# The unit norm of the delta rule's queries, taken at the output norm

## The reference, cut to what matters

```python
def rms_norm(x, w):
    xf = x.astype(jnp.float32)
    y = xf * lax.rsqrt(jnp.mean(xf * xf, axis=-1, keepdims=True) + NORM_EPS)
    return (y * w.astype(jnp.float32)).astype(x.dtype)

def l2_normalize(x):
    xf = x.astype(jnp.float32)
    return xf * lax.rsqrt(jnp.sum(xf * xf, axis=-1, keepdims=True) + NORM_EPS)
...
    qkv = jax.nn.silu(causal_dwconv(qkv, qkv_conv))
    q, k, v = [...]
    o = gated_delta_rule_chunked(l2_normalize(q), l2_normalize(k), v, g, beta)
    o = rms_norm(o, o_norm) * jax.nn.silu(z...)
...
    qc = chunks(q) * (dk ** -0.5)        # in the delta rule: the only use of q
    attn = jnp.einsum('nbhik,nbhjk->nbhij', qc, kc) * decay
    ...
        o_c = (jnp.einsum('bhck,bhkv->bhcv', q_c * jnp.exp(g_c)[..., None], state)
               + jnp.einsum('bhij,bhjv->bhiv', attn_c, v_new))
```

## Time and profile before

| | |
|---|---|
| median of 3 runs | 2117.26 us (2116.29 to 2118.51) |
| profiled execution | 2116.69 us, span of its trace 2114.8 us |
| TensorE busy | 2092.3 us, 99% |
| VectorE busy | 920.9 us, 44% |
| ScalarE busy | 921.0 us, 44% |
| GpSimd busy | 755.5 us, 36% |
| granted TensorE clock | 9 of 9 in all 40 slices |

### The profile page before, as it was taken

The page is one execution under the profiler, slowest core; times in us unless marked ns, Lnnn a source line. Parts: engine busy times, 40 slices in busy tenths (PEclk is TensorE's granted clock), DMA queues, the critical chain, the costliest instruction groups (busy, mean ns, idle before and its releaser), DMA issues.

```text
span 2114.8 us, 28556 instructions
## 1 busy us (share of the span) xinstructions
PE 2092.3 (99%) x11044; PEld 1641.3 (78%) x11044; DVE 920.9 (44%) x1399; ACT 921.0 (44%) x1425; POOL 755.5 (36%) x316
## 2 busy tenths in 40 slices
PE   8999999999999999999999999999999999999999
PEld 5777788888888885668888888777688887867887
DVE  7875551112137157755111213654633354464331
ACT  7642453323245327764332323564643244565221
POOL 3331244444444620004444444433044444302443
PEclk9999999999999999999999999999999999999999
DMA  4432133333333420003333333222023332202232
GB/s 154 139 116 72 42 104 100 93 99 97 91 99 98 146 84 21 2 26 92 99 98 99 90 97 98 87 74 84 1 84 95 93 97 80 82 19 60 90 91 89
DMA packets 62708, 178.95 MB, mean 85 GB/s; under 512 B 17776, under 2 KB 18160, under 8 KB 62592
## 3 DMA queue, kind: packets, MB, share of 16 engines
q1 hardware_dynamic: 47600, 168.04, 26.1%
q10 hardware_dynamic: 14992, 9.22, 1.6%
HBM read 171.97 MB, written 3.70 MB: 83 GB/s over the span
## 4 chain that ended last, share of the span: by engine, by line
issue 47%; PE 34%; POOL 16%; ACT 1%; POOLq 0%; DMA 0%; SPq 0%; DVE 0%
POOL w_lo L2655 16%; PE banks L749 9%; PE banks L751 9%; PE banks L750 9%; PE banks L1251 2%; PE banks L1263 1%; ACT probT L1903 1%; PE banks L1255 1%; PE banks L800 1%; PE banks L1276 1%; PE banks L1228 0%; DMA x<-in_x 0%; PE banks L1312 0%; POOLq L2661 0%; POOLq L2663 0%
## 5 line engine op out<-in xcount | busy, mean ns | idle before, releaser
L2655 POOL TENSOR_TENSOR w_lo<-raw,w_hi 128x1024 fp32r<-128x1024 f32 (+1 forms) x312 | 755.3, 2422 | 1342.8 <-ACT w_hi L1397 1342.7
L749 PE MATMUL banks<-h_lo,w_hi 128*128 128x512 f32 (+1 forms) x1408 | 566.3, 402 | 8.7 <-POOL w_lo L2655 8.7
L751 PE MATMUL banks<-h_hi,w_hi 128*128 128x512 f32 (+1 forms) x1408 | 555.2, 394 | 0.0
L750 PE MATMUL banks<-h_hi,w_lo 128*128 128x512 f32 (+1 forms) x1408 | 552.0, 392 | 0.0
L1397 ACT ACTIVATE w_hi<-raw 128x1024 fp32r<-128x1024 f32 (+1 forms) x312 | 327.9, 1051 | 491.8 <-PE banks L751 458.5
L749 PEld LDWEIGHTS banks<-h_lo,w_hi 128*128 128x128 f32 (+1 forms) x1408 | 264.5, 188 | 75.4 <-issue 10.3
L750 PEld LDWEIGHTS banks<-h_hi,w_lo 128*128 128x128 f32 (+1 forms) x1408 | 264.4, 188 | 62.7 <-issue 5.0
L751 PEld LDWEIGHTS banks<-h_hi,w_hi 128*128 128x128 f32 (+1 forms) x1408 | 264.4, 188 | 59.9 <-issue 0.7
L749 PE MATMUL banks<-a_lo,w_hi 128*128 128x512 f32 x768 | 303.0, 395 | 0.0
L751 PE MATMUL banks<-a_hi,w_hi 128*128 128x512 f32 x768 | 302.4, 394 | 0.0
L750 PE MATMUL banks<-a_hi,w_lo 128*128 128x512 f32 x768 | 300.5, 391 | 0.0
(11 more groups left out here) (344 smaller groups left out, 2411.9 us busy)
## 6 DMA issues: line engine op xcount, KB each, us to landing
raw<-in_weights SPq DMA_DIRECT2D x311, 512.0 KB, 3.5
x<-in_x SPq DMA_DIRECT2D x4, 512.0 KB, 6.1
AT<-row_dram ACTq DMA_DIRECT2D x4, 512.0 KB, 7.5
out<-x SPq DMA_DIRECT2D x8, 256.0 KB, 2.0
eg<-row_dram ACTq DMA_DIRECT2D x8, 128.0 KB, 3.2
phase<-in_phase ACTq DMA_DIRECT2D x1, 706.0 KB, 4.4
phase<-in_phase ACTq DMA_DIRECT2D x1, 704.0 KB, 4.1
ld_dram<-Ld ACTq DMA_DIRECT2D x1, 512.0 KB, 5.4
```

The costliest lines, as they stand in the source:

```text
L749: mm(out, w_hi, x_lo, start=first, stop=False)
L750: mm(out, w_lo, x_hi, start=False, stop=False)
L751: return mm(out, w_hi, x_hi, start=False, stop=last)
L2655: return nc.gpsimd.tensor_tensor(c.w_lo[:, slot, 0:n], c.raw[:, slot, 0:n], c.w_hi[:, slot, 0:n].bitcast(F32), ALU.subtract)
```

## The change

The queries are no longer scaled. The four sums `("l2", 0)` to `("l2", 3)`, their four roots with the table loads, and their four scalings on VectorE are gone. In the places of the four squares ScalarE now squares the raw queries, times a constant, into a new buffer `q_sq` (three tiles; the fourth goes to a free half of `norm`). In the chunk loop VectorE adds these squares to the output's squares in `sq` before TensorE sums them, in two additions (`add_query_squares`), and TensorE's sum waits for the semaphore `on_added` instead of for ScalarE's square (`out_sum`). The constant is folded into the squares and into the bias of the logarithm.

```diff
-    (13, 0): [("l2", 0)], (13, 4): [("l2", 1)], (16, 0): [("l2", 2)], (16, 4): [("l2", 3)],
...
-ROOTS_AT = {4: (4, 1), 6: (6, 3), 14: (0, 5), 17: (2, 7)}
+ROOTS_AT = {4: (4, 1), 6: (6, 3)}
...
+    c.q_sq, _ = put("q_sq", [P, 3, T], o)
...
+    def out_sum(ch):
+
+        i = sums[0]
+        out = claim(("on", ch))
+        pe.wait_ge(c.on_added, ch + 1)
+        mm(out[:, :], k0["blk64"], c.sq[:, i % 2, :], start=True, stop=True).then_inc(c.sq_used, 1)
+        sums[0] += 1
...
-        sum_squares(("on", ch - 1), k0["blk64"])
+        out_sum(ch - 1)
...
+    def query_square(i):
+
+        read(("qkv", i))
+        f(query_squares(c, i), c.qkv[:, i, :], ACT.Square, scale=ON_EPS_ROOT).then_inc(c.q_sq_ready, 1)
...
-            head_square(0)
-            head_square(1)
+            query_square(0)
+            query_square(1)
...
-        if t in (14, 17):
-            head_roots(ROOTS_AT[t][0], ROOTS_AT[t][0] + 1)
         if t == 14:
-            head_square(2)
-            head_square(3)
+            query_square(2)
+            query_square(3)
...
-        stt(y, y, GDN_D ** -0.5 if i < 4 else 1.0, c.psum[bank[key][0]][:, :], ALU.mult, ALU.mult).then_inc(release(key), 1)
+        tt_op(y, y, c.psum[bank[key][0]][:, :], ALU.mult).then_inc(release(key), 1)
...
+    def add_query_squares(ch):
+
+        n = GDN_K_TILES + ch
+        dve.wait_ge(c.sq_ready, n + 1)
+        cols, total = slice(ch * P, ch * P + P), tiles_of(c.sq[:, n % 2, :], 4)
+        tt_op(total[:, 0:3, :], total[:, 0:3, :], c.q_sq[:, :, cols], ALU.add)
+        tt_op(total[:, 3, :], total[:, 3, :], query_squares(c, 3)[:, cols], ALU.add).then_inc(c.on_added, 1)
...
     dve.wait_ge(c.s_clear, 1)
+    dve.wait_ge(c.q_sq_ready, 4)
+    v.memset(c.tiny[:, 40:41], ON_EPS_ROOT ** 2 / GDN_D * EPS).then_inc(c.on_eps_ready, 1)
     for ch in range(NT):
         if ch:
+            add_query_squares(ch - 1)
             key = ("ws", ch)
             tt_op(tiles_of(c.vnew[:, :], 4), c.u[:, :, ch * P:ch * P + P], tiles_of(filled(key)[:, :], 4), ALU.subtract)\
...
+    add_query_squares(NT - 1)
     add_to_x(("outb", NT), NT)
...
+def query_squares(c, i):
+
+    return c.q_sq[:, i, :] if i < 3 else c.norm[:, 1, :]
```

More of the change, by code:

```diff
@@ L39 @@
 GDN_H, GDN_D = 8, 64
+GDN_K_TILES = GDN_H * GDN_D // P
+ON_EPS_ROOT = GDN_D * EPS ** 0.5
 NSA_H, NSA_D, NSA_G = 16, 64, 4
@@ L292, in scratch_bank @@
     if key[0] == "l2":
-        return (4 if key[1] < 4 else 6) + key[1] % 2
+        return 6 + key[1] % 2
     if key[0] == "kk1":
@@ L550, in place @@
     c.e_row, o = put("e_row", [P, T], o)
+    o += 4 * T
     c.tok, o = put("tok", [P, 8, 32], o)
@@ L675, in add_semaphores @@
     c.l2_root = sem("l2_root")
+    c.on_eps_ready = sem("on_eps_ready")
+    c.q_sq_ready = sem("q_sq_ready")
+    c.on_added = sem("on_added")
     c.on_root = sem("on_root")
@@ L862, in grams @@
         if name == "qk":
-            read(("l2", p))
+            read(("qkv", p))
         for t in chunks:
@@ L1032, in program_tensor @@
     short_half(NT)
-    sum_squares(("on", NT - 1), k0["blk64"])
+    out_sum(NT - 1)
     for m in range(NT + 1, KT):
@@ L1675, in step_root @@
     def step_root(ch):
-        log_mean(c.on_r[:, :], ("on", ch), GDN_D)
-        read(("on", ch))
+        key = ("on", ch)
+        count["used"] += 1
+        act.wait_ge(c.sq_used, count["used"])
+        f(c.on_r[:, :], c.psum[bank[key][0]][:, :], ACT.Ln, bias=c.tiny[:, 40:41], scale=1.0 / GDN_D).then_inc(release(key), 1)
+        read(key)
         f(c.on_r[:, :], c.on_r[:, :], ACT.Exp, scale=-0.5).then_inc(c.on_root, 1)
     passed("outb", 0)
+    act.wait_ge(c.on_eps_ready, 1)
     square(filled(("o", 0))[:, :])
@@ L2600, in program_vector @@
                 add_to_x(("out2", l, m), m)
+def query_squares(c, i):
+    return c.q_sq[:, i, :] if i < 3 else c.norm[:, 1, :]
 def squares_before(l):
-    return 8 + 4 + l * (4 + 1 + 4 + 6)
+    return GDN_K_TILES + 4 + l * (4 + 1 + 4 + 6)
 def build(nc, in_x, in_weights, in_common, in_phase0, in_phase1, in_phase2, in_params, out):
```

## The result

The changed kernel takes 2125.64 us (median of seven executions, 2121.08 to 2127.54), the kernel before 2117.26 beside it (seven, 2116.29 to 2119.22). The ratio is 1.0033, 95% interval 1.0024 to 1.0043: slower, by more than the 0.2% that can be told apart. The forecast was 2119.3 us with a range up to 2122.5, so it missed. The profiled execution took 2124.64 us, 7.95 more than the 2116.69 of before.

A forecast was written before the change was run, and what follows sets the result against it. TensorE's own queue, busy for 99% of the span, was taken as the bound. A kept lead of -3.9 and waits of 0, 3.3, 1.1 and 2.1 gave +2.6 us on 2116.69, so 2119.3 us; range 2114.2 to 2122.5.

The forecast's parts named there:

- what goes from TensorE: Tiles 13 and 16: four float32 products of squares go, leaving TensorE 5.2 us ahead at the end of tile 16.
- the way round through memory: Before `X,MT`: the inverse, written to memory and fetched back, makes TensorE wait about 1.3 us, leaving 3.9 of the gain.
- from there to the chunk loop the exchanges of the four head pairs are paced by TensorE, and the lead is carried along: From `X,MT` of pair 0 to the chunk loop: no further loss, the lead of 3.9 us is kept.
- that the second addition is blocked, and how long TensorE waits for it: Chunk loop: GpSimd blocks the second addition at sums 2 and 4; waits of 0, 3.3, 1.1 and 2.1 us.
- the sum took the clock at nothing: Chunk loop: the total of +2.6 us held no term for a slower TensorE clock behind the new stalls.
- rival C in its farther form: Chunk loop: the 3.3 and 2.1 us stalls both cost TensorE its clock, 2122.9 us; chance of C 0.15.
- the deciding idle time: TensorE's stalls in the chunk loop: the idle time from which the clock falls, put between 1.6 and 3.3 us.
- the forecast's +2.6: Whole kernel: predicted net change in us against the profiled execution of before, 2116.69 us, giving 2119.3 us.

The follow-up runs named there:

- Experiment 8: Experiment 7 with the masked kk product of pair 0 (`MT`) made earlier on VectorE: 2113.4 us, ratio 0.9977.
- Experiment 4: Changed kernel with three, one and two extra products, results overwritten, keeping TensorE busy before sums 2, 3 and 4: 2121.27 us, ratio 1.0015.
- experiment 6: Changed kernel with three extra products, results overwritten, before sum 2 alone: 2123.14 us, ratio 1.0021.
- Experiment 7: Changed kernel with additions right behind `step_norm`, and pair 2's decay copy and query scaling moved behind the copies completing `X` and `XT`: 2113.04 us, ratio 0.9976.
- experiment 3: Changed kernel with the two additions swapped, 128x128 ahead of 128x384, in the same place: 2117.69 us, ratio 1.0.
- experiment 2: Changed kernel without the additions, TensorE's sum waiting for ScalarE's square; the query's term is left out: 2113.3 us, ratio 0.9977.
- experiment 5: Kernel before, all query norms kept, plus two additions of the same shapes (of the gate's `z`) in the same place: 2127.02 us, ratio 1.0043.
- experiments 1: Changed kernel with the two additions right behind `step_norm`, two instructions earlier: 2114.95 us, ratio 0.9986.

## Why the prediction was wrong, step by step

**Right: what goes from TensorE.** 5.4 us in the trace for 5.2 (4.6 to 5.6 in the other traces with the removal).

**Right, by a bound near enough: the way round through memory.** `X,MT` of pair 0 starts at 148.02, forecast near 147.7, and the lead there is 3.6 us for 3.9. Experiment 8 shows that this is the bound. Three parts of the working were off and partly cancelled. VectorE's inverse was done 0.7 us earlier (its last copy starts at 136.41 for 137.07), where 1.2 had been forecast, so the split of `yb` 0 came later than forecast too (142.74 for 142.2). But the write landed in 3.6 us instead of the 5.1 of the earlier trace rows, so that the split alone set the start of the fetches, at 142.81.

**Failed: "from there to the chunk loop the exchanges of the four head pairs are paced by TensorE, and the lead is carried along".** It wasn't: 1.3 us were lost at pair 2. VectorE's copy of the decays, a small instruction, had started 0.5 us ahead of GpSimd before (192.48 and 192.98). Now it came 0.8 us after GpSimd had started, and took 1.59 us, to GpSimd's end, in front of what `X,MT` needs. In the traces of experiments 4 and 6 it came only 0.17 and 0.03 us after GpSimd's start, took 2.23 and 2.37 us, and TensorE waited 2.41 and 2.55. I had read where VectorE has time in hand, but not what a shift by 3.6 us does to its meetings with GpSimd. Experiment 7 shows the cause, by removing it: the wait is back at 0.5 us.

**Right: that the second addition is blocked, and how long TensorE waits for it.** The waits were 3.1, 1.0 and 1.9 us for 3.3, 1.1 and 2.1, and none at sum 1. The kernel before already had such a block right behind sum 2 (`Sd`, 2.89 us, experiment 3), nearer than the that I went by. The additions take 0.55 and 0.28 us for 0.56 and 0.30. The Trainium skill (SBUF — State Buffer, "Who interferes with whom") leaves open which engine gets the port between two VectorE instructions; here it was GpSimd, at both sums, and with 0.20 us instead of 0.47 between the two starts (experiment 3) it no longer came in between.

**Failed: the sum took the clock at nothing.** The clock fell behind the stalls of sums 2 and 4, 1.6 us each: rival C in its farther form, with 3.2 us for my 3.6. This step alone took the time out of the range: 2125.6 less 3.2 is 2122.4, while 2125.6 less pair 2's 1.3 is still 2124.3. I gave it 0.15 and left it at the range's edge. Experiment 4 shows it apart from the waits. I had set the deciding idle time between 1.6 and 3.3 us, and both of my forecast stalls, 2.1 and 3.3, lay in or at the end of that interval; a price of 1.8 for each with an even chance would have stood in the sum as 1.8 us, and the range would have had to reach 2123. The Trainium skill (TensorE: Matmul & The Clock Gate, "Part 1: The HAM clock gate") says that an idle TensorE loses half its clock; these two stalls, of 3.13 and 1.90 us, were enough for it.

**Not in the sum: small terms.** 0.4 us before chunk 2's product with `S`. It waits for VectorE's new `S`, which starts 1.51 us after TensorE's product for it instead of 1.15. Its cause is open: VectorE had been idle for 4.00 us by then, so the additions ahead of it in its queue don't explain it, and neither experiment 2 nor experiment 5 has this wait. And there are 0.24 us at each stalled sum beyond its wait (1.23 later for 0.99 at sum 3), 0.7 in all.

The accounts: -5.4 for the sums that went; +1.8 up to `X,MT` of pair 0, where 1.3 had been forecast; +1.3 at pair 2; +0.4; 6.0 of waits, where 6.5 had been forecast; 3.2 for the clock; 0.7. Together +8.0, in the trace +8.1. Of the 5.5 us between the trace and the forecast's +2.6, 3.2 are the clock's and 1.3 pair 2's. The median of all executions is 1.0 us above the profiled one, whose mean granted clock, 0.998, is not the lowest (three of the seven have 0.997).

## What to carry to other kernels

Before work is added to VectorE's queue in front of something that the busiest engine waits for, look for the place where its inputs are ready and not for the place where its result is due: here the same two additions cost 10 us in one place, and two instructions earlier no sum waits for them (2115.0 us, for 2113.3 without them, both with executions down to 2112.8 or below). Where GpSimd and VectorE both work on SBUF, ask for every instruction that moves, however small, what GpSimd runs at its new time; two short instructions in a row are a gap that it can enter, and the order of the two can decide. And price a new stall of the bottleneck not by its length alone: behind seven of the nine idle times of 1.8 us or more in these traces the clock fell (the start of the program left out), and so it is a second term, to be put into the sum with a chance and not left to a rival.

## What was not expected of the hardware

- **The stall's length alone doesn't decide whether the clock falls.** The granted clock fell behind idle times of 3.13 us (twice: the changed kernel and experiment 5), 2.55 (experiment 6), 1.90 and 1.89 at sum 4 (the changed kernel, experiments 5 and 6) and 1.82 (experiment 2). It did not behind 2.41 at pair 2 in experiment 4, behind 1.80 at tile 16 in experiment 5, behind 1.78 at pair 2 in the changed kernel and in experiments 1 and 3, nor behind the 1.55 of before. So between 1.8 and 2.4 us both happen, even at one place (pair 2). What else decides is open; executions of one kernel differ in it, and their times with them.
- **The price differed by place.** Behind sums 2 and 4 it was 1.6 us. At pair 2, among the small products of the inverse, it was 3.1 us in experiment 2 and 4.3 in experiment 6, where the clock stayed at the lower level longer (0.50 from 200 to 205 us in both). Whether that comes from the products behind the stall or from something else wasn't tried.
- **A small instruction is blocked as long as a large one.** A copy of four columns took 1.59 us (0.16 alone), an addition of 128x128 took 2.43 (0.28 alone): both end within 0.2 us of GpSimd's end. Passes with an operand in PSUM in the place of the copy were not held (0.69 us, experiment 7).
